# The last weight loads held behind the experts' rows, and the router's logits made with its matrix as the weights

## What is computed

```python
def moe_swiglu(x, router_w, w1, w3, w2):
    logits = (xt @ router_w).astype(jnp.float32)
    top_vals, top_idx = lax.top_k(logits, TOP_K)
    gates = jax.nn.softmax(top_vals, axis=-1)
    combine = jnp.sum(one_hot(top_idx) * gates[..., None], axis=1)
    for e in range(N_EXPERTS):
        out = out + combine[:, e:e + 1] * swiglu(xt, w1[e], w3[e], w2[e])
...
    h = h + moe_swiglu(f, router_w[j], moe_w1[j], moe_w3[j], moe_w2[j])
    gate = jax.nn.sigmoid(rmsnorm(h, ple_norm_g[i]) @ ple_gate_w[i])
    h = h + gate * (p[i] @ ple_proj_w[i])
```

## Time and profile before

| | |
|---|---|
| median of three runs | 1708.97 us |
| the profiled execution | 1711.69 us |
| its span on the core | 1709.8 us |
| PE busy | 1695.3 us (99%) |
| DVE busy | 1378.6 us (81%) |
| ACT busy | 1231.2 us (72%) |
| POOL busy | 59.2 us (3%) |
| DMA from 740 to 1675 us, nearly all of the eight rounds | 382 GB/s |

### The profile page before, as it was taken

The page is one execution under the profiler, slowest core; times in us unless marked ns, Lnnn a source line. Parts: engine busy times, 40 slices in busy tenths (PEclk is TensorE's granted clock), DMA queues, the critical chain, the costliest instruction groups (busy, mean ns, idle before and its releaser), DMA issues.

```text
span 1709.8 us, 24926 instructions
## 1 busy us (share of the span) xinstructions
PE 1695.3 (99%) x8555; PEld 1415.4 (83%) x8555; DVE 1378.6 (81%) x1607; ACT 1231.2 (72%) x1564; POOL 59.2 (3%) x43
## 2 busy tenths in 40 slices
PE   9999999999999999999999999999999999999998
PEld 7877779898888889888888888888888888888786
DVE  5667876777774577699899898899898998989995
ACT  6667665665553566887888887887877878878775
POOL 0002100000000000000000000000000000000301
PEclk9999999999999999999999999999999999999999
DMA  9942354369645453299999999999999999999993
GB/s 320 345 182 95 110 193 172 123 227 419 247 179 215 154 203 148 105 393 380 373 397 372 376 386 372 379 397 365 385 386 376 388 375 370 402 370 386 380 375 123
DMA packets 76948, 510.60 MB, mean 299 GB/s; under 512 B 8312, under 2 KB 8440, under 8 KB 19537
## 3 DMA queue, kind: packets, MB, share of 16 engines
q1 hardware_dynamic: 67792, 479.45, 72.3%
q0 software_dynamic: 6496, 25.52, 4.6%
q10 hardware_dynamic: 2592, 4.72, 0.7%
HBM read 485.02 MB, written 24.64 MB: 298 GB/s over the span
## 4 chain that ended last, share of the span: by engine, by line
PE 94%; DVE 2%; DMA 1%; ACT 1%; issue 1%; ACTq 0%; SPq 0%; POOL 0%; DVEq 0%; POOLq 0%
PE ps L1990 23%; PE ps L1995 22%; PE ps L1991 22%; PE ps L2397 6%; PE ps L1954 4%; PE ps L2404 3%; PE ps L2376 1%; PE ps L2375 1%; PE ps L2382 1%; PE ps L1983 1%; PE ps L1975 1%; PE ps L1979 1%; DVE wlo L1271 1%; DMA raw<-in_w_fixed_dram 1%; PE ps L2291 1%
## 5 line engine op out<-in xcount | busy, mean ns | idle before, releaser
L1271 DVE TENSOR_TENSOR wlo<-raw,whi 128x1024 fp32r<-128x1024 f32 x886 | 1028.1, 1220 | 130.3 <-ACT whi L760 129.2
L760 ACT ACTIVATE whi<-raw 128x1024 fp32r<-128x1024 f32 x886 | 882.4, 1053 | 119.5 <-PE ps L1995 84.6
L1990 PE MATMUL ps<-whi,xgh 128*128 128x512 f32 x896 | 353.6, 395 | 0.0
L1991 PE MATMUL ps<-whi,xgl 128*128 128x512 f32 x896 | 348.9, 389 | 0.0
L1995 PE MATMUL ps<-wlo,xgh 128*128 128x512 f32 x896 | 276.7, 390 | 1.6 <-DVE wlo L1271 1.5
L1995 PEld LDWEIGHTS ps<-wlo,xgh 128*128 128x128 f32 x896 | 167.9, 188 | 38.2 <-DVE wlo L1271 2.8
L1990 PEld LDWEIGHTS ps<-whi,xgh 128*128 128x128 f32 x896 | 168.3, 188 | 34.2 <-ACT whi L760 0.4
L1991 PEld LDWEIGHTS ps<-whi,xgl 128*128 128x128 f32 x896 | 168.4, 188 | 33.4
L1990 PE MATMUL ps<-whi,mTh 128*128 128x512 f32 x448 | 175.9, 393 | 0.0
L1991 PE MATMUL ps<-whi,mTl 128*128 128x512 f32 x448 | 174.4, 389 | 0.0
L1995 PE MATMUL ps<-wlo,mTh 128*128 128x512 f32 x448 | 138.1, 389 | 0.0
(11 more groups left out here) (418 smaller groups left out, 1952.6 us busy)
## 6 DMA issues: line engine op xcount, KB each, us to landing
raw<-in_w_moe_dram SPq DMA_DIRECT2D x336, 1024.0 KB, 7.2
raw<-in_w_fixed_dram SPq DMA_DIRECT2D x112, 1024.0 KB, 5.1
tokens_scratch<-zeros POOLq DMA_DIRECT2D x1, 8704.0 KB, 44.6
y_scratch<-zeros POOLq DMA_DIRECT2D x2, 2304.0 KB, 57.6
y_scratch<-yo ACTq DMA_DIRECT2D x18, 256.0 KB, 6.0
xin<-tokens_scratch SPq DMA_DIRECT2D x8, 512.0 KB, 7.3
bias_scratch<-revb POOLq DMA_DIRECT2D x1, 3072.0 KB, 38.1
raw<-in_w_fixed_dram SPq DMA_DIRECT2D x4, 512.0 KB, 4.6
```

The source lines that it names most:

```text
L760: AC(whi[:, v % SPL, c], raw[:, v % RAW, c], ACT.Copy).then_inc(high_done, 1)
L1271: V.tensor_tensor(wlo[:, v % SPL, c], raw[:, v % RAW, c], whi[:, v % SPL, c].bitcast(F32), ALU.subtract).then_inc(low_done, 1)
L1990: mm(o, hi(k0 + k, T), wh[:, k, :], start=first and k == 0, stop=False)
L1991: mm(o, lo(k0 + k, T), wh[:, k, :], start=False, stop=False)
```

## The change

Line numbers of the changed kernel are higher by up to 7. There are seven edits:

- the router's logits: `rw` is now the weights (128x8), and the 256 tokens of `router_x` are streamed. The logits come out as 8 rows of 256; DVE copies them to SBUF (into `pick`, which is free then), PE turns them back behind `late_p(0, 1)`, and DVE copies the result to `lg`;
- the lower experts' rows: POOL only fetches them; DVE scales and adds them in the last round, in two instructions between its splits;
- row block 0 of `y_scratch`: POOL clears it in the dense stage with the other blocks, from `zeros`; ACT no longer stores it and only counts the semaphores up;
- SP waits for `y_fetched[0]` before it loads the last four units;
- DVE's `add_last(1)` stands ahead of the split of unit 44, and the low part of the second turned tiles ahead of that of unit 45;
- on PE, `second_rows` stands before the last four matmuls of unit 43 (those with the low part of the data), and the four matmuls that no one read are gone;
- the counts that wait for the clearing go from 48 to 80.

```diff
+            sp.wait_ge(y_fetched[0], 32)
             for j, unit in enumerate(after):
                 load(U["ple1"] + j, unit)
...
+                        pool.dma_start(y_dram[half][0:1].rearrange("a p n -> p (a n)"), zeros[:, 0:NB])\
+                            .then_inc(rows_cleared, 16)
...
-            pool.wait_ge(low_fetched, 64)
-            for T in range(NT):
-                ins = pool.tensor_scalar(y_low[:, T, :], y_low[:, T, :], gk[:, 0, T:T + 1], None, ALU.mult)
-            ins.then_inc(low_scaled, 1)
-            pool.wait_ge(low_scaled, 1)
-            pool.tensor_tensor(h[:], h[:], y_low[:], ALU.add).then_inc(low_added, 1)
...
-            act.wait_ge(y_copied, 2)
             for half in range(2):
-                store(half, 0)
+                act.sem_inc(rows_stored[half], 16)
...
                 else:
+                    for T in range(NT):
+                        dve.wait_ge(low_fetched, 64)
+                        V.scalar_tensor_tensor(out=h[:, T, :], in0=y_low[:, T, :], scalar=gk[:, 0, T:T + 1],
+                                               in1=h[:, T, :], op0=ALU.mult, op1=ALU.add).then_inc(low_added, 1)
+                        split_to(ub + 4 * NFB + 6 + T + AHEAD)
                     split_to(ub + UNITS_ROUND - 1)
-                    dve.wait_ge(low_added, 1)
+                    dve.wait_ge(low_added, 2)
                     add_last(0)
...
                 ub, bb = U["ple1"], B["ple1"]
+                add_last(1)
                 split_to(ub + 2)
-                add_last(1)
+                turned_low(6, 1)
                 split_to(ub + 3)
-                turned_low(6, 1)
                 invert_root(6)
...
-            step(V.tensor_copy(lg[:].rearrange("p t e -> p (t e)"), ps[:, 4, 0:NT * NE]))
+            V.tensor_copy(logit_rows, ps[0:NE, 4, 0:S]).then_inc(logits_copied, 1)
+            dve.wait_ge(router_logits, 2)
+            step(V.tensor_copy(lg[:].rearrange("p t e -> p (t e)"), ps[:, 5, 256:256 + NT * NE]))
...
+                        if half and before_low:
+                            before_low()
                         pe.wait_ge(low, n_parts)
...
-                products(ub + 1, KU, NB, *X, 0, outs[1], True, False)
-                second_rows()
-                for _ in range(4):
-                    mm(ps[:, 6, :], order[:, 1, :], whi[:, (ub + 1) % SPL, 0:NB], start=True, stop=True)
+                products(ub + 1, KU, NB, *X, 0, outs[1], True, False, norm=6, before_low=second_rows)
...
-                    for T in range(NT):
-                        ins = mm(ps[:, 4, T * NE:(T + 1) * NE], router_x[:, k, T * P:(T + 1) * P], rw[:, k, :],
-                                 start=k == 0 and T == 0, stop=k == KD - 1, skip_group_check=True)
+                    ins = mm(ps[0:NE, 4, 0:S], rw[:, k, :], router_x[:, k, :], start=k == 0, stop=k == KD - 1)
             ins.then_inc(router_logits, 1)
             late_p(0, 1).then_inc(p_late_made, 1)
+            pe.wait_ge(logits_copied, 1)
+            for T in range(NT):
+                ins = turn(ps[:, 5, 256 + T * NE:256 + (T + 1) * NE], logit_rows[:, T * P:(T + 1) * P],
+                           ident[0:NE, 0:NE])
+            ins.then_inc(router_logits, 1)
             late_p(1, 0).then_inc(p_late_made, 1)
```

More of the change, by code:

```diff
@@ L320, in build @@
         y_last = tok
+        logit_rows = pick[0:NE].rearrange("p t n -> p (t n)")
         warm = qT[:, 0, :]
@@ L360, in build @@
         low_fetched = sem("low_fetched")
-        low_scaled = sem("low_scaled")
         low_added = sem("low_added")
@@ L446, in build @@
         router_logits = sem("router_logits")
+        logits_copied = sem("logits_copied")
         sel_done = sem("sel_done")
@@ L694, in _ @@
                             .then_inc(rows_cleared, 16)
+                        pool.dma_start(y_dram[half][0:1].rearrange("a p n -> p (a n)"), zeros[:, 0:NB])\
+                            .then_inc(rows_cleared, 16)
             pool.wait_ge(router_logits, 1)
             pool.memset(yo[:], 0.0).then_inc(y_copied, 2)
-            pool.wait_ge(rows_cleared, 48)
+            pool.wait_ge(rows_cleared, 80)
             pool.wait_ge(rows_ready, 1)
@@ L777, in root @@
                 if k == 3:
-                    act.wait_ge(rows_cleared, 48)
+                    act.wait_ge(rows_cleared, 80)
                 for i in range(NT):
@@ L1630, in mix @@
                 if i:
-                    dve.wait_ge(rows_cleared, 48)
+                    dve.wait_ge(rows_cleared, 80)
                 if i == 0:
@@ L1959, in split_view, with products @@
                         wlo[:, s, 0:nk * n].rearrange("p (k n) -> p k n", k=nk))
-            def products(u, nk, n, hi, lo, k0, outs, first, last, middle=None, halves=(0, 1), norm=None):
+            def products(u, nk, n, hi, lo, k0, outs, first, last, middle=None, halves=(0, 1), norm=None,
+                         before_low=None):
                 wh, wl = split_view(u, nk, n)
```

## The result

The changed kernel takes 1713.68 us, median of 16 runs, against 1710.55 us for the kernel before in 16 runs beside them: a ratio of 1.0019, 95% interval 1.0013 to 1.0026. It is 3.2 us **slower**, where 2.65 us faster was forecast. On the scale of the prediction, 1708.97 us, that is 1712.2, outside its range. The profiled execution took 1713.42 us with a span of 1711.3, 1.5 more than before's span.

What follows compares the result with a forecast made beforehand. PE hardly stands still in the rounds, so only its few waits and the chain behind its last expert unit count. -1.5 - 0.8 - 0.65 + 0.3 = -2.65 us takes 1708.97 to 1706.3 us; 8-in-10 range 1703.9 to 1710.8.

Steps and rivals of the forecast that it cites:

- POOL's addition: Last round: with POOL's arithmetic moved to DVE, PE's 1.5 us wait for DVE's split goes; -1.5 us (0 to -1.8).
- ACT's stores: Ahead of round 0: two stores, 0.91 us, go from before ACT's first split; -0.8 us (0 to -0.9).
- Router: Router stage: the clock stays at 2.4 GHz, so PE counts at 719.87 instead of 720.52; -0.65 us.
- The held loads: Last units: SP loads after the fetched rows; PE's 2.3 us wait becomes 4.2 us; +0.3 us (-1.5 to +4.9).
- The clock ahead of unit 42: Rival: PE's 4.2 us wait before unit 42 drops the clock; 1.0 us of it shows, 1707.3 us; chance 0.09.
- The hold costs more than it gives: Rival: before unit 42, rows land late for a reason other than loads; 4.85 replaces 0.3, 1710.9 us; chance 0.15.

Runs made afterwards that it cites:

- the kernel with the loads free: Changed kernel without SP's wait for the fetched rows, all other parts kept: 1708.69 us, ratio 0.9992 to the kernel before.
- the early additions: Changed kernel, hold included, with DVE's two additions of the low rows some 45 us earlier in the last round: 1710.49 us.
- the busy PE: Changed kernel with 26 more matmuls of 512 columns, result unread, on PE ahead of unit 42: 1711.67 us.
- addition alone: Kernel before with POOL's addition moved to DVE as the only edit: 1709.87 us, ratio 1.0003 to the kernel before.
- hold alone: Kernel before with SP's wait for the fetched rows as the only edit: 1713.29 us, ratio 1.0022 to the kernel before.
- DVE quiet: Changed kernel with DVE made to wait for POOL's first two fetch issues ahead of the splits of the last three units: 1709.60 us.

## Why the prediction was wrong

- **POOL's addition** (-1.5): right in the trace; no split over 1.3 us, no wait. PE gains 1.8 us there, from 1.06 ahead of before at 740 us to 2.82 behind 1608 us. That DVE would fall behind was seen (by 1.4 us in the sum), and weighed for PE only.
- **ACT's stores** (-0.8): right; the break at 733 is gone. It measures about 0.5 us there and 0.9 by 740 us, with the matmuls behind it.
- **Router** (-0.65): the clock stays at 1.00, as forecast, but `lg` is copied 1.9 us later, not 1.6, and the count stands at 720.21 where it stood at 720.52. Against the profile of before that is 0.4 us by the turns; against the mean of six old ones nothing. The step that failed is to take the fallen clock of the earlier trace rows for every execution.
- These three together: forecast -2.95, measured -2.85 by PE's row of unit 41, in the profiled executions. That the sum fits so well is luck in part, since the router gives only 0.2 of its 0.65 and the other two more than forecast. In the medians the kernel with the loads free gains 1.6.
- **The held loads** (+0.3, from -1.5 to +4.9): this is the term that was mis-sized. It is 5.0 us in the medians. Right were the rows 2.6 us behind POOL's second issue (measured 2.7: 1669.03 to 1671.77), the first load in 4.7 us (4.8), the next 2.5 us later (2.6). Two steps failed. "POOL is through with the second issue" was taken with the issues of the kernel before, 2.09 and 1.95 us, while the first part of the same change moved the additions to where they make the first one long: 3.2 us, by the early additions. And the matmuls of units 42 and 43 were taken at full clock behind the wait: 2.0 us, by the busy PE. Together 5.2, and 5.5 with the forecast's own 0.3, against 5.0; no run has both remedies at once. In the profile the steps of the chain up to the second rows stand within some 0.3 us of the times in the sum (SP's loads at 1671.79 for 1671.7, the second rows added from 1690.70 for 1690.8), but this is chance: those times are counted in the kernel before, and PE was 2.85 us ahead of it. The longer issue used that up, and the 1.5 us that were lost beyond it came with the clock.
- **The rivals.** The clock ahead of unit 42 fell, with a chance of 0.09 on record and a price of 1.0; it fell in all four kernels with the full hold and an idle PE. "The hold costs more than it gives" named the right sign, but by rows that land late for their distance from POOL's issue; they landed in time, the issue itself was late. So each of the two causes had its like among the rivals, taken one at a time; both came together.

## What to carry to other kernels

Work that is moved to an engine because it has slack can hold up another one that does not wait for it, as DVE's two additions did POOL's issue (2.09 us before, 5.93 after): ask it of every engine that runs beside, not only of those that wait for it. Before a load is held for a short fetch, see that what PE needs next is already in: here two units held instead of four turned 3.2 us lost into 4.3 won. And before a stall of one profiled execution goes into a sum, look whether the kernel's runs spread by more than that stall.

## What the runs showed of the hardware

- An indirect fetch of POOL took 0.95 us to issue with DVE idle; 3.2 us beside two of DVE's two-input subtractions; and in the last round 0.95 to 2.09 us where DVE's run of them followed a wait of 1.43 us or more, 5.4 to 6.5 us where it followed the additions without one. The Trainium skill (SBUF — State Buffer, Who interferes with whom) infers that such a subtraction leaves descriptor generation alone; the five long issues, which last until DVE's run is nearly over, speak against that, though no run shows which access waits.
- Behind PE's waits of 2.4 and 2.5 us (loads free, addition alone) four matmuls took 1.07 us, at a granted clock of 1.00; behind 3.9 to 6.3 us (hold alone, DVE quiet, additions early, changed kernel) they took up to 2.05 us, at 0.50 to 0.54, close to the lower level of 1.2 GHz.
- The same 32 router matmuls with 8 streamed columns ended at either clock, in executions whose program is the same up to there. What decides it stays open.
